# Dealing token slots over the partitions, a first load in halves and an earlier copy in a decoder block with 32 experts

## What is computed

```python
g_logits = ht @ w_group + b_group                   # 4 groups, best one
e_logits = ...                                      # 8 experts of that group, best two
...
hg = silu(einsum('td,edf->tef', ht, w1[g])) * einsum('td,edf->tef', ht, w3[g])
out = out + einsum('tef,efd->td', hg * combine[:, g, :, None], w2[g])
```

## Time and profile before

| what | us |
|---|---|
| runs before, median (lowest, highest) | 619.59 (618.88, 620.04) |
| the profiled execution, its own time | 618.37 |
| its span, first to last instruction | 616.4 |

### The profile page before, as it was taken

One profiled execution on the slowest core, in us unless ns is written; L12 is line 12 of the kernel. 1 busy time (PEld: TensorE's weight loads), 2 busy tenths in 40 slices (PEclk: granted clock), 3 DMA queues, 4 the chain that ended last, 5 costly groups with the idle time before them and its releaser, 6 DMA issues.

```text
span 616.4 us, 7800 instructions
## 1 busy us (share of the span) xinstructions
PE 543.3 (88%) x3018; PEld 342.6 (56%) x3018; DVE 297.9 (48%) x523; ACT 184.3 (30%) x328; POOL 79.1 (13%) x101
## 2 busy tenths in 40 slices
PE   1689999999988999999999848899998999878797
PEld 1577768778766666665446524455544445434443
DVE  4988674366889736661032664233222223312216
ACT  5265562343454458872042211000000000000002
POOL 8132100000000000000041111112111111200000
PEclk9989999999999999999999869999999999999999
DMA  8987855495253074002920497999999999999957
GB/s 335 400 256 261 310 189 213 157 387 207 68 206 103 1 288 190 1 2 77 425 112 34 188 366 261 409 417 421 420 419 419 419 418 422 419 420 423 401 233 290
DMA packets 42626, 169.28 MB, mean 275 GB/s; under 512 B 7848, under 2 KB 9896, under 8 KB 30308
## 3 DMA queue, kind: packets, MB, share of 16 engines
q1 hardware_dynamic: 32356, 140.81, 57.3%
q0 software_dynamic: 9104, 25.95, 11.9%
q10 hardware_dynamic: 1136, 2.11, 0.9%
HBM read 160.74 MB, written 16.25 MB: 287 GB/s over the span
## 4 chain that ended last, share of the span: by engine, by line
PE 62%; DMA 13%; DVE 9%; SPq 8%; ACT 4%; issue 2%; DVEq 0%; POOLq 0%; ACTq 0%
PE banks L1833 11%; PE banks L1712 9%; PE banks L1853 5%; DMA qkT<-in_w_dram 5%; DMA obuf<-in_w_dram 4%; PE banks L1547 4%; PE banks L1549 4%; PE banks L1548 4%; PE banks L1664 3%; DMA stage<-in_w_in_dram 3%; PE banks L1648 2%; PE banks L1541 2%; PE banks L1539 2%; PE banks L1540 2%; SPq L455 2%
## 5 line engine op out<-in xcount | busy, mean ns | idle before, releaser
L859 ACT ACTIVATE work<-banks 128x256 f32<-128x256 f32 x16 | 6.1, 384 | 198.4 <-PE banks L1833 198.4
L1853 PE MATMUL banks<-stage,work 128*64 128x512 f32 x168 | 58.3, 598 | 6.3 <-ACT work L861 6.3
L1833 PE MATMUL banks<-qkT,work 128*64 128x256 f32 x272 | 61.5, 381 | 0.3 <-DMA stage<-in_w_dram 0.3
L1712 PE MATMUL banks<-stage,mixT 128*128 128x512 f32 x128 | 56.2, 594 | 0.0
L1356 DVE TENSOR_TENSOR work<-banks,gates 128x1024 f32<-128x1024 f32 x15 | 18.4, 1225 | 72.7 <-PE banks L1853 72.7
L1350 DVE TENSOR_TENSOR work<-work,banks 128x256 f32<-128x256 f32 x16 | 6.7, 422 | 87.4 <-ACT work L859 87.4
L1833 PE MATMUL banks<-hT,work 128*64 128x256 f32 x192 | 43.2, 381 | 2.8 <-DMA qkT<-in_w_dram 2.8
L1549 PE MATMUL banks<-hT_hi,w_lo 128*128 128x512 f32 x112 | 43.8, 391 | 0.0
L899 DVE SCALAR_TENSOR_TENSOR mixT<-stage,small,mixT 128x1024 f32<-128x1024 f32 x32 | 41.0, 1282 | 0.6
L1547 PE MATMUL banks<-hT_hi,w_hi 128*128 128x512 f32 x96 | 40.4, 421 | 0.0
L1712 PEld LDWEIGHTS banks<-stage,mixT 128*128 128x128 f32 x128 | 24.0, 190 | 28.9 <-issue 28.9
(11 more groups left out here) (304 smaller groups left out, 1156.4 us busy)
## 6 DMA issues: line engine op xcount, KB each, us to landing
stage<-in_w_dram SPq DMA_DIRECT2D x31, 1024.0 KB, 20.3
qkT<-in_w_dram SPq DMA_DIRECT2D x23, 1024.0 KB, 23.8
stage<-in_w_ada_dram POOLq DMA_DIRECT2D x16, 1024.0 KB, 5.7
hT<-in_w_dram SPq DMA_DIRECT2D x12, 1024.0 KB
stage<-in_w_in_dram SPq DMA_DIRECT2D x5, 2048.0 KB, 11.2
val<-in_w_dram SPq DMA_DIRECT2D x10, 1024.0 KB
mixT<-in_w_dram SPq DMA_DIRECT2D x10, 1024.0 KB
alibi<-in_w_dram SPq DMA_DIRECT2D x5, 1024.0 KB
```

What stands on the lines that cost most here:

```text
L1712: ins = mm(banks[:, w % 5, :], mixT[:, k, t * P:(t + 1) * P], wv[:, k % 4, half * 512:(half + 1) * 512], start=(k == 0), stop=(k == KD - 1))
L1833: ins = mm(banks[half * C:(half + 1) * C, 2, up * F:(up + 1) * F], heT[:, r, k * P + half * C:k * P + (half + 1) * C], ws[2 * place + half ...
L1853: ins = mm(banks[half * C:(half + 1) * C, 4 + 2 * r + col, :], geT[:, fc * P + half * C:fc * P + (half + 1) * C], w2s[2 * place + half][:, ...
```

## The change

There are three edits.

1. `slot_neg` holds another order of the numbers 0 to 127. Partition 32a + 4e + 2r + d (a = 0 to 3, e = 0 to 7, r and d = 0 or 1) gets slot 32a + 16r + e when d is 0 and slot 32a + 16r + 15 - e when d is 1. So slots 0 to 7 of an expert go one each to the eight groups of four neighbouring partitions, slots 8 to 15 again one each in reverse order, and so on. It takes two iota instructions in place of one.
2. For the first load of the expert stage (w1 of pair 3 into place 0), each 1 MB transfer is issued as two of 512 KB. The first halves wait for a new semaphore that PE raises after half of the k steps of pair 0's w1, the second halves for `h1_done`. Pairs 3 to 5 are now loaded by code outside of SP's loop. PE waits once for `w1_early` before its loop.
3. The copy of the last token tile (L1262 before) comes ahead of `best_of_each` for the third tile, and 4 more matmuls without a use (`fill(4, FILLERS_LOGITS)`) are put on PE between the last tile's transposes and the first ranks.

```diff
+FILLERS_LOGITS = 4
...
+                load_down(e0, e1, place, up_free, down_free)
+
+            def load_down(e0, e1, place, up_free, down_free):
...
-            with sp.Fori(0, NQ // R - 1) as it:
+            for part in range(2):
+                cut = slice(part * F * KD // 2, (part + 1) * F * KD // 2)
+                sp.wait_ge(h1_done if part else h1_part, 1)
+                for n in range(2):
+                    sp.dma_start(slots[n][0][:, cut], w1_v[2 * R + n][:, cut]).then_inc(w1_in[0] if part else w1_early, 16)
+            load_down(2 * R, 2 * R + 1, 0, 1, 1)
+            for n in range(1, R):
+                load_pair(2 * (n + R), 2 * (n + R) + 1, n, n + 1, n + 1)
+            with sp.Fori(1, NQ // R - 1) as it:
...
-            link(g.iota(slot_int, pattern=[[-1, P]], base=0, channel_multiplier=0))
+            fours = slot_int.rearrange("p (a e r d) -> p a e r d", a=4, e=8, r=2)
+            g.iota(fours[:, :, :, :, 0], pattern=[[-32, 4], [-1, 8], [-16, 2]], base=0, channel_multiplier=0)
+            link(g.iota(fours[:, :, :, :, 1], pattern=[[-32, 4], [1, 8], [-16, 2]], base=-15, channel_multiplier=0))
...
-            best_of_each(NT - 2, NT - 1)
             dve.wait_ge(fT_done, NT)
             dve.wait_ge(logits_done, NT - 2)
             v.tensor_copy(x2T[:, (NT - 1) % 2, 0:512], banks[:, 6, :]).then_inc(x2T_ready, 1)
+            best_of_each(NT - 2, NT - 1)
...
             pe.wait_ge(y_scaled, 2 * NT)
+            fill(4, FILLERS_LOGITS)
             pe.wait_ge(masks_ready, 1)
...
+                    if first and k == KD // 2 - 1:
+                        ins.then_inc(h1_part, 1)
...
+            pe.wait_ge(w1_early, 32)
             with pe.Fori(0, (NQ - 4) // 6) as it:
```

More of the change, by code:

```diff
@@ L304, in hymba_block @@
         rows_zero = sem("rows_zero")
-        h1_done = sem("h1_done")
+        h1_done, h1_part, w1_early = sem("h1_done"), sem("h1_part"), sem("w1_early")
         first_half = sem("first_half")
@@ L1785, in _, with fill @@
                 out_proj(t + 5)
+            def fill(bank, count):
+                for n in range(count):
+                    mm(banks[:, bank, :], ones_bf[:], ones_bf[:].unsqueeze(1).to_broadcast([P, NT, P]),
+                       start=True, stop=True)
             def ranks_of(j):
@@ L1826, in expert_T, with expert_up @@
                 ins.then_inc(eT_done, 1)
-            def expert_up(arrived, ws, up, place, value, r):
+            def expert_up(arrived, ws, up, place, value, r, first=False):
                 pe.wait_ge(arrived[place], value)
@@ L1835, in expert_up, with expert_h @@
                                  start=(up + k == 0), stop=(k == KD - 1), skip_group_check=True)
-                return ins
-            def expert_h(n, place, value, r):
-                expert_up(w1_in, w1s, 0, place, value, r).then_inc(h1_done, 1)
+                    if first and k == KD // 2 - 1:
+                        ins.then_inc(h1_part, 1)
+                return ins
+            def expert_h(n, place, value, r, first=False):
+                expert_up(w1_in, w1s, 0, place, value, r, first).then_inc(h1_done, 1)
                 expert_up(w3_in, w3s, 1, place, value, r).then_inc(h_done, 1)
@@ L1888, in rows_of @@
                 return rows_in[q % 2], more + 16 * (q // 2 + 1)
-            for n in range(FILLERS):
-                mm(banks[:, 7, :], ones_bf[:], ones_bf[:].unsqueeze(1).to_broadcast([P, NT, P]), start=True, stop=True)
+            fill(7, FILLERS)
             pe.wait_ge(scatter_ready, 1)
             expert_T(None, rows_of(0), 0)
-            for n in range(FILLERS_BETWEEN):
-                mm(banks[:, 7, :], ones_bf[:], ones_bf[:].unsqueeze(1).to_broadcast([P, NT, P]), start=True, stop=True)
+            fill(7, FILLERS_BETWEEN)
             expert_T(None, rows_of(1), 1, 6)
@@ L1898, in _ @@
             pe.wait_ge(heT_ready, 1)
-            expert_h(1, 0, turn(0), 0)
+            expert_h(1, 0, turn(0), 0, True)
             expert_geT(1)
```

## The result

The changed kernel runs in **612.16 us** (median of 4 runs, 611.53 to 612.27); the kernel before ran in 619.72 beside it (4 runs). The ratio is 0.988, its 95% interval 0.9854 to 0.9906, which is 5.8 to 9.0 us. The forecast was 613.2 us, from 610.8 to 616.6. The profiled execution took 612.15 us with a span of 610.2; before they were 618.37 and 616.4, so these two differ by 6.2 us, where the sum said 6.35. The medians differ by 1.3 us more than that, which is less than their interval.

The account below looks back on a forecast made before the run. Weights were taken to wait for the DMA engine with the most gather and scatter rows. Gains of 5.0 + 0.85 + 0.5 = 6.35 us from 619.59 gave 613.2 us, range 610.8 to 616.6.

Parts of the forecast that it names:

- The bound, and where the queue runs out: Expert stage: weights wait for the last DMA engine, 6.4 us behind the mean once the queue is empty.
- Part 1, 5.0 us: Expert weight stream: the new slot order takes 42 rows from the last engine, gaining 5.0 us (4.6 to 6.6).
- The price of 0.12 us a row: Gathers and scatters: cost of one row, taken between 0.11 us (tail) and 0.156 us (stream's rate).
- Part 3, the shift 0.45 us earlier: Router: the earlier copy starts the last tile's `add_shift` 0.45 us earlier (0.2 to 0.65).
- The gather 0.4 us shorter: First gather: its fullest engine carries 5 or 6 rows instead of 8, saving 0.4 us (0 to 1.0).
- Part 2, 0.5 us: First expert load in halves: starts 1.85 us earlier, of which 0.5 us stays (0 to 1.1).
- The sum: Whole kernel: 5.0 + 0.85 + 0.5 = 6.35 us gained, median 613.2 us.
- PE becomes the bound: Expert stage: the stream's gain passes PE's limit, so the gain is 8.35 us, 611.2 us; chance 0.15.
- A slow engine: Engine of partitions 28 to 31 and 60 to 63 slow by itself; 3 us slower gives 616.2 us; chance 0.15.
- The deal doesn't do what it says: Indirect DMA engines not bound to those partitions: the slot order gives nothing, 618.2 us; chance 0.10.
- The clock: PE's clock stays at half through pair 0, stream up to 14 us later, about 627 us; chance 0.05.
- What was to show it: Signs: DMA share falls within 3 to 5 us, w3 of pair 14 at 568 to 570, first halves near 372.8.

Follow-up runs that it names:

- e2_no_deal: The changed kernel with the slots in order again, halves and router edits kept: 618.79 us, ratio 0.9981 to the kernel before.
- e4_no_rows: The changed kernel with every gather and scatter index out of bounds, so no row of a pair is moved: 609.6 us, ratio 0.9819 to the kernel before.
- e8_mirrored: The changed kernel with the deal of slots reversed, so the most rows lie on partitions 0 to 3 and 32 to 35: 612.6 us.
- e1_deal_only: The kernel before with the new order of the slots and nothing else: 613.27 us, ratio 0.9891 to the kernel before.
- e5_halves_only: The kernel before with the first load in halves and nothing else: 618.6 us, ratio 0.9981 to the kernel before.

## Why the prediction was right, step by step

**The bound, and where the queue runs out.** Right. The argument from the slope of the earlier trace rows, that the weights wait for one engine behind the others, is borne out from both sides: e2_no_deal brings the slope back, e4_no_rows takes the wait away. The Trainium skill (DMA: Bandwidth & Descriptors, The descriptor swizzle) gives the grouping of four partitions and the four that lie 32 higher. The runs agree with it, in indirect transfers too: the same rows piled on such groups cost 630.33 us, spread over them 612.16.

**Part 1, 5.0 us.** Right: 5.06 us of D with the deal alone, 4.73 when it is undone. The price of 0.12 us a row, chosen between 0.11 and 0.156, measured 0.113 in this step. It was right as a number, and for this step only: 0.08 to 0.18 by the load. The reason given for it, that the tail shows what a row costs these engines, doesn't hold: a row took 0.161 us on its engine before and after, near the upper bound. That D moved by only 0.11 us a row has no explanation in the runs, so choosing near the lower bound was in part luck. The second iota cost nothing that can be seen: VectorE still had 1.77 us idle ahead of its product, 2.13 before.

**Part 3, the shift 0.45 us earlier.** The term that was mis-sized. S fell by 0.25 us, within the 0.2 to 0.65 but at its low end. The step that failed is that VectorE's sequence would slip by 0.4 to 0.7 us into 1.06 us of idle time. It slipped by 0.81, and the idle time was itself a product of the clock in that one execution, which the prediction saw and yet took as given.

**The gather 0.4 us shorter.** 5.64 us after 5.82, 0.18 less. The term was sized as if rows made the gather long, and with no rows at all it still takes 4.99. From the third tile's shift to pair 0's w1 the two terms together are 23.89 - 23.47 = 0.42 us, where 0.85 stood in the sum. The w1 came 0.61 us earlier; the other 0.2 us were there ahead of the router (347.51 against 347.70).

**Part 2, 0.5 us.** Between 0.2 and 0.7 by D, and not to be told from none in the time with the deal in place. The reason given, that the next w1 can't be issued before PE has done its pair, is what SP's queue shows. The pause that this leaves came at 376 to 380 us, and not before 391.

**The sum.** 6.35 forecast, 6.2 by the two profiled executions: stream 5.28 (of 5.5), lead 0.61 (of 0.85), and 0.31 behind the stream, mostly a shorter pause that stood in no term. The errors partly cancel. The median fell by 7.6 us, with an interval of 5.8 to 9.0, and the 6.35 lies inside.

**The rivals.** *PE becomes the bound*: no, PE still waits for three weights, 2.0 us in all, and its limit is 2.4 us further; the prediction had 2.0 left. (It put the limit 7.5 us under the kernel before at w3 of pair 14; e4_no_rows has 7.7.) *A slow engine*: excluded by e8_mirrored for the engine that was named, beyond some 0.8 us. *The deal doesn't do what it says*: excluded by e1_deal_only. *The clock*: full from 366 us on in the changed kernel; a small case of it stood in e5_halves_only, 1.3 us.

**What was to show it.** The share ends within 5 us, w3 of pair 14 at 569.48 (568 to 570), pair 12 runs without a wait for a weight, the first half at 372.97: all as written. The shift (0.25 for 0.45) and pair 0's w1 (0.61 for 0.85) fell short.

## What to carry to other kernels

When a stream of large transfers shares its engines with a small irregular one, the mean DMA share hides the imbalance; look at how long the share takes to fall once the queue is empty, since the area under that slope tells how far the last engine is behind. Here 6.4 us were read from it, and dealing the irregular work evenly over the groups of partitions gave 5.1. Move an operation ahead on an engine only if it doesn't wait there for longer than what it overtakes takes: five small operations that fill a wait are free. And before costing an idle time of a few tenths of a us, ask whether the clock made it, since one profile can't say.

## What the runs showed that I had not expected

- A row of 4 KB takes its engine 0.16 us whatever the load, but costs the stream 0.08, 0.13 or 0.18 us by how loaded the fullest engine is (122 to 136, to 164, to 224 rows). Neither the lower nor the higher price is explained.
- The granted clock fell at a different moment of the same router work from one profile to another: within 350 to 352 us in that of before, within 352 to 354 in that of e1_deal_only, whose router is the same. Worth 0.8 us between the two shifts (5.07 against 4.26), and nothing that was seen at the end.
- An issue of the first gather that comes 0.6 to 0.9 us earlier bought nothing; the gather took that much longer.
- PE idle for 3.50 us ahead of the first pair was followed by a clock of 0.50 for some 2 us, and cost 1.3 us in that profile. After 3.38 us at the same place in another the clock stayed at 1.00.
